# Latent chunks ahead of context chunks in one input norm, one-pass factors for the mixer's two norms, and column sums kept in one bank

## What is computed

```python
def rms_norm(x, g):
    y = xf * lax.rsqrt(jnp.mean(xf * xf, axis=-1, keepdims=True) + EPS)
    return (y * g).astype(x.dtype)
# second layer
h_lat = modulate(rms_norm(lat, norm1_g[1]), sh1, sc1)
h_ctx = modulate(rms_norm(cx, norm1_g[1]), csh1, csc1)
z_lat = h_lat @ w_in                       # queries need latents only
kv_ctx = h_ctx @ w_in[:, C_Q_LORA:]        # keys and values need both
...
return rms_norm(lat, final_g)              # end of the first block ("final1")
...
h = rmsnorm(x, norm_mix_g[0])              # start of the second ("mix"), x being that result
proj = h @ w_in[0]
```

## Time and profile before

| | us |
|---|---|
| median of 3 runs | 1631.31 (1631.01 to 1636.09) |
| the profiled execution | 1633.56 |
| its span, first to last instruction | 1631.7 |
| PE busy in it | 1535.8 (94%) |
| DVE busy | 1126.5 (69%) |
| ACT busy | 797.4 (49%) |
| mean granted TensorE clock | 0.973 |

### The profile page before, as it was taken

How to read it: one execution, slowest core, us unless ns; L and a number is a source line. 1 busy time by engine, 2 the same in 40 slices (tenths; PEclk the granted TensorE clock), 3 DMA queues, 4 the chain that set the end, 5 groups by cost and what they waited for, 6 DMA issues and landing times.

```text
span 1631.7 us, 31148 instructions
## 1 busy us (share of the span) xinstructions
PE 1535.8 (94%) x11566; PEld 1355.6 (83%) x11566; DVE 1126.5 (69%) x1853; ACT 797.4 (49%) x1437; POOL 122.9 (8%) x139
## 2 busy tenths in 40 slices
PE   5899988899899999999899999999999889999998
PEld 3688878787688888878786799999898669999997
DVE  5986866544798888887735478875666755577653
ACT  2545554243544545322445567765445455666542
POOL 2000052512000000010000010001000001000000
PEclk8999999899899999999899999999899999999999
DMA  9354520002244445566431045556454214255552
GB/s 368 108 180 164 186 66 2 3 2 78 94 177 170 165 166 179 174 213 217 173 110 52 5 151 190 183 197 214 144 168 143 84 59 143 92 191 182 186 188 90
DMA packets 62957, 230.80 MB, mean 141 GB/s; under 512 B 6800, under 2 KB 8080, under 8 KB 62352
## 3 DMA queue, kind: packets, MB, share of 16 engines
q1 hardware_dynamic: 61408, 223.37, 39.5%
q0 software_dynamic: 1168, 5.80, 1.0%
q10 hardware_dynamic: 288, 0.33, 0.1%
HBM read 228.43 MB, written 1.05 MB: 141 GB/s over the span
## 4 chain that ended last, share of the span: by engine, by line
PE 85%; DVE 8%; ACT 4%; issue 2%; DMA 1%; POOL 1%; DVEq 0%; ACTq 0%; POOLq 0%
PE proj L662 23%; PE proj L663 23%; PE proj L664 23%; PE bank L714 1%; PE bank L925 1%; DVE w_low L2165 1%; ACT w_high L1647 1%; PE proj L1145 1%; DMA ident_sb<-ident 1%; PE bank L942 1%; PE bank L972 1%; POOL tmp L1516 1%; PE proj L1147 1%; PE proj L1146 1%; PE bank L1160 1%
## 5 line engine op out<-in xcount | busy, mean ns | idle before, releaser
L662 PE MATMUL proj<-h_high,w_high 128*128 128x256 f32 (+1 forms) x1776 | 583.0, 328 | 19.9 <-DVE h_low L2198 13.5
L663 PE MATMUL proj<-h_low,w_high 128*128 128x256 f32 (+1 forms) x1776 | 572.0, 322 | 0.0
L664 PE MATMUL proj<-h_high,w_low 128*128 128x256 f32 (+1 forms) x1776 | 570.6, 321 | 0.0
L2165 DVE TENSOR_TENSOR w_low<-w_raw,w_high 128x1024 fp32r<-128x1024 f32 x322 | 393.3, 1224 | 152.9 <-ACT w_high L1647 151.5
L1647 ACT ACTIVATE w_high<-w_raw 128x1024 fp32r<-128x1024 f32 x322 | 337.9, 1054 | 232.0 <-PE proj L664 228.0
L662 PEld LDWEIGHTS proj<-h_high,w_high 128*128 128x128 f32 x1776 | 337.2, 190 | 56.5 <-issue 18.4
L664 PEld LDWEIGHTS proj<-h_high,w_low 128*128 128x128 f32 x1776 | 337.8, 190 | 27.2
L663 PEld LDWEIGHTS proj<-h_low,w_high 128*128 128x128 f32 x1776 | 337.5, 190 | 24.4
L662 PE MATMUL proj<-act_high,w_high 128*128 128x256 f32 (+1 forms) x608 | 190.6, 313 | 0.1
L663 PE MATMUL proj<-act_low,w_high 128*128 128x256 f32 (+1 forms) x608 | 189.7, 312 | 0.0
L664 PE MATMUL proj<-act_high,w_low 128*128 128x256 f32 (+1 forms) x608 | 189.3, 311 | 0.0
(11 more groups left out here) (413 smaller groups left out, 1911.2 us busy)
## 6 DMA issues: line engine op xcount, KB each, us to landing
w_raw<-w_stream SPq DMA_DIRECT2D x322, 512.0 KB, 3.3
a_ring<-a_stream SPq DMA_DIRECT2D x80, 512.0 KB, 4.1
a_first<-a_head SPq DMA_DIRECT2D x4, 1024.0 KB, 18.0
a_first<-a_stream SPq DMA_DIRECT2D x4, 1024.0 KB, 18.6
x<-x_in SPq DMA_DIRECT2D x1, 2048.0 KB, 10.3
late_tab<-late_tables POOLq DMA_DIRECT2D x1, 1408.0 KB, 6.6
cond_rows<-cond_rows SPq DMA_DIRECT2D x1, 1024.0 KB, 5.6
cond_rows<-cond_rows POOLq DMA_DIRECT2D x1, 1024.0 KB, 5.1
```

Of the source, the lines that this page charges most:

```text
L662: mm(out_, wh, xh, start=first, stop=False)
L663: mm(out_, wh, xl, start=False, stop=False)
L664: return mm(out_, wl, xh, start=False, stop=last)
L2165: v.tensor_tensor(wl(n), RAW[:, n % 4, :], wh(n), ALU.subtract).then_inc(w_low, 1)
```

## The change

**n1_1 by stream.** `norm_parts` lists 16 parts for the names in `BY_STREAM` (only n1_1): eight latent chunks, then eight context chunks, each of 256 columns, with a count of their own. Tiles 0 to 2 wait for the latents only, tile 3 waits for each context chunk. On ACT block in1+2 is split ahead of the root, and tile copies and splits stand between the context chunks. On DVE the `w_low` of in1+2 follows context chunk 0 and that of in1+3 follows context chunk 4 (`beside`). POOL's load of `mem_in` waits for all 16.

**One bank of sums.** `norm_sum` puts the columns of all token groups side by side in one bank, only the very first matmul opening the accumulation, and `norm_root` takes one square root over the 2 or 4 columns, for every norm.

**The mixer's factor.** With s the mean of x squared, the two factors together are 1/sqrt(mean(x²·(g²+eps)) + eps²), g being `final1`'s weight. So ACT squares x scaled by sqrt(g²+eps), held in eight new columns of `small` that two linked ACT instructions make at the start of dn1, and both factors become a root and a reciprocal each, without the other. PE sums chunk by chunk for both names (`mix` in bank 0, `final1` in bank 2) and spreads them apart, `mix` into bank 0 and `final1` into bank 1, with a signal each. The first index logits of in2_v, which use bank 1, wait until `X` is scaled. Column `eps_squared` fills the padding of `cols_sb`; `small` grows from 72 to 88 columns, so every buffer behind it lies 64 bytes higher.

```diff
-            for t in range(width // P):
-                last = f(STD[:, t:t + 1], SUMS[t][:, 0:1], ACT.Sqrt, scale=1.0 / features, bias=col("eps"))
-            last.then_inc(n_root, 1)
+            nt = width // P
+            f(STD[:, 0:nt], BK[0][:, 0:nt], ACT.Sqrt, scale=1.0 / features, bias=col("eps")).then_inc(n_root, 1)
...
+        def norm_parts(name):
+            nch = NORMS[NORM_I[name]][1]
+            if name in BY_STREAM:
+                return [(k, [part]) for part in ((LAT, 1), (CTX, 0)) for k in range(nch)]
+            return [(k, streams(name)) for k in range(nch)]
...
             norm_start("mix" if then == "final1" else then)
+            if then == "final1":
+                link(f(SM[:, 72:80], C[:, COL_AT["final1"]:COL_AT["final1"] + KC], ACT.Square))
+                link(f(SM[:, 72:80], SM[:, 72:80], ACT.Sqrt, bias=col("eps")))
...
-            if then != "final1" and then not in UNSCALED:
+            if then in BY_STREAM:
+                split(B0["in1"] + 2)
+                norm_root(then)
+                norm_high(then, range(KC))
+            elif then != "final1" and then not in UNSCALED:
                 norm_end(then)
...
-        split(B0["in1"] + 2)
+        norm_high("n1_1", range(KC, KC + 3))
         for m, o in enumerate([CQ[:, 0, :], CQ[:, 1, :], CQ[:, 2, :], CKV[:, 0, :], CKV[:, 1, :], KR[:]]):
             split(B0["in1"] + m + lead("in1"))
+            if m == 2:
+                norm_high("n1_1", range(KC + 4, 2 * KC))
             done(T0["in1"] + m)
             f(o, PL[(T0["in1"] + m) % 2][:, 0:o.shape[1]], ACT.Copy).then_inc(tile_out, 1)
+            if m == 0:
+                norm_high("n1_1", range(KC + 3, KC + 4))
...
-            norm("n1_1")
-            low(B0["in1"] + 2)
-            rest("in1", 0, 4)
+            norm("n1_1", lambda j: low(B0["in1"] + 2 + (j > KC)) if j in (KC, KC + 4) else None)
+            rest("in1", 1, 4)
...
-            norm_sum("mix", 1, 0)
-            norm_sum("final1", 0, 2)
-            pe.wait_ge(n_std, NORM_I["mix"] + 2)
+            norm_sum("mix", "final1")
+            for c, name in enumerate(("mix", "final1")):
+                pe.wait_ge(n_std, NORM_I[name] + 1)
...
+                    if c == 0:
+                        pe.wait_ge(n_xn, NORM_X0["final1"] + KC)
...
-            for t in range(2):
-                last = v.scalar_tensor_tensor(STD[:, 16 + t:17 + t], SUMS[t][:, 1:2], STD[:, 8 + t:9 + t], STD[:, 8 + t:9 + t], ALU.mult, ALU.mult)
```

More of the change, by code:

```diff
@@ L42 @@
         ("a_ln_g", 4), ("a_ln_b", 4), ("b_norm", 1), ("mla_q", 3), ("mla_kv", 2), ("fconv", 2 * 2 * FC * 3),
-        ("final1", 8), ("mix", 8), ("kv2", 1), ("cross", 8), ("mem", 8), ("mlp", 8), ("final2", 8), ("eps", 1), ("one", 1)]
+        ("final1", 8), ("mix", 8), ("kv2", 1), ("cross", 8), ("mem", 8), ("mlp", 8), ("final2", 8), ("eps", 1), ("one", 1), ("eps_squared", 1)]
 COL_AT = {}
@@ L88 @@
 UNSCALED = ("cross", "mlp")
+BY_STREAM = ("n1_1",)
 NORM_X0 = {}
 NORM_C0, NORM_S0 = {}, {}
-_c = _s = 0
+_c = _s = _x = 0
 for _name, _nc, _ in NORMS:
-    NORM_C0[_name], NORM_S0[_name] = _c, _s
-    NORM_X0[_name] = _c - sum(n for m, n, _ in NORMS[:NORM_I[_name]] if m in UNSCALED)
+    NORM_C0[_name], NORM_S0[_name], NORM_X0[_name] = _c, _s, _x
+    _parts = 2 * _nc if _name in BY_STREAM else _nc
     _c += _nc
-    _s += _nc if _name in SPLIT else 0
+    _x += 0 if _name in UNSCALED else _parts
+    _s += _parts if _name in SPLIT else 0
 A_FIRST = 16
@@ L672, in free_bank, with tile @@
                 pe.wait_ge(tile_out, t + 1 + off)
-            def tile(n, t, x, width, off=0):
+            def tile(n, t, x, width, off=0, ready=None):
                 weights(n, off)
@@ L700, in h_ready, with norm_sum @@
                 return lambda k: (n_lo, NORM_S0[name] + k + 1)
-            def norm_sum(name, c=0, count=1):
-                _, nch, width = NORMS[NORM_I[name]]
-                chunks = [0, *range(EARLY, nch)] if name in SUMMED else range(nch)
+            def norm_sum(*names):
+                _, nch, width = NORMS[NORM_I[names[0]]]
+                early = names[0] in SUMMED
+                chunks = [0, *range(EARLY, nch)] if early else range(nch)
                 for k in chunks:
-                    if name in SUMMED and k == 0:
-                        pe.wait_ge(n_early, (EARLY - 1) * (SUMMED.index("final1" if name == "mix" else name) + 1))
-                    else:
-                        pe.wait_ge(n_sq, sq_count(name, k))
-                    for t in range(width // P):
-                        last = mm(SUMS[t][:, c:c + 1], squares(name, k)[:, t * P:(t + 1) * P], ONES[:, 0:1], start=(k == 0), stop=(k == nch - 1))
-                if count:
-                    last.then_inc(n_ss, count)
+                    for c, name in enumerate(names):
+                        if early and k == 0:
+                            pe.wait_ge(n_early, (EARLY - 1) * (SUMMED.index(names[-1]) + 1))
+                        else:
+                            pe.wait_ge(n_sq, sq_count(name, k))
+                        for t in range(width // P):
+                            o = BK[2 * c][:, t:t + 1]
+                            last = mm(o, squares(name, k)[:, t * P:(t + 1) * P], ONES[:, 0:1], start=(k == 0 and t == 0), stop=(k == nch - 1 and t == width // P - 1))
+                        if k == nch - 1:
+                            last.then_inc(n_ss, 1)
             def norm_spread(name):
@@ L1103, in _ @@
                 x = LAT if m < 3 else slice(0, T2)
-                tile(B0["in1"] + m, T0["in1"] + m, x, SEQ if m < 3 else T2)
+                ready = (lambda k: (n_lo, NORM_S0["n1_1"] + KC + k + 1)) if m == 3 else None
+                tile(B0["in1"] + m, T0["in1"] + m, x, SEQ if m < 3 else T2, ready=ready)
                 if m == 3:
@@ L2202, in low_part @@
                     last.then_inc(n_lo, 1)
-                for k in range(nch):
+                for j, (k, own) in enumerate(parts):
                     src = norm_src(name, k)
```

78 lines of the change are left out of this document (39 added, 39 removed).

## The result

The changed kernel takes 1636.84 us (1635.69 to 1638.18, 8 runs) against 1631.16 (1627.79 to 1636.09, 8 runs) for the kernel before: ratio 1.0032, 95% interval 1.0019 to 1.0044. That is 5.7 us slower, where 8.9 us faster was forecast. The profiled execution took 1635.69 us; its span is 1633.9.

The account below looks back on a forecast made before the run. TensorE, 85% of the chain, was taken as the bound, other engines counting only where it waits. Terms -0.42 - 0.42 - 4.1 - 0.22 + 0.45 - 4.2 = -8.9 us gave 1622.4 us on the median, range 1619 to 1628.5.

Parts of the forecast that it names:

- n1_1: Second layer's input norm: order by stream starts projections and third tile earlier; 4.1 us gain, root's 0.42 included, bounds 1.5 to 4.9.
- One bank of sums: All norms: column sums put into neighbouring columns of one bank cost nothing, bound 0.02 us a pass either way.
- The mixer: Mixer's norms: sums, root and spread finish sooner, so scaling starts earlier; 4.2 us gain, bounds 2.5 to 5.3.
- the address shift: Rival, all projections: activations 64 bytes higher might slow matmuls; at 1% 6.5 us slower than before, 1637.8; chance 0.08.
- One root: Norms: one root for four or two saves 0.42 us at n1_0, n2_0, n1_1 each, 0.11 at n2_1, final2 each.
- The queue of ScalarE: At n1_1: copy behind rounding and split starts third tile at 805.2; rival: handovers delay it near 808, chance 0.12.
- The rival with the halved clock: At n1_1's third tile: clock halves in the pause, so n1_1 gains only 2.0 us, total 1624.5; chance 0.20.
- Start of dn1: Two added small ScalarE instructions, covered by nothing, delay TensorE by 0.45 us, bounds 0.2 to 0.7.
- The new wait in in2_v: First index logits wait until `X` is scaled; VectorE's work covers it by 2.1 us, so it costs nothing.

Follow-up runs that it names:

- two distances: Unshifted changed kernel with ScalarE's tile 0 copy earlier, `w_high` at distance 0 ahead of in1 and 192 from in1 on; 1614.65 us, ratio 0.9899 to before.

## Why the prediction was wrong, step by step

**The step that failed** is the one that left the address shift out of the sum. It stood among the rivals, with the right quantity in it (slower from 0.6% per matmul on), and got 0.08 because no row showed a price and the alignment stayed legal. "No row shows it" was true of the trace of before, but bounds were due on either side: the range, 1619 to 1628.5, was added up from the bounds of the other terms, and no slower case lies in it. The page of the changed kernel shows how much hangs on the operands' place, and that of before had the same counts (one of three such groups for each operand; x the number of matmuls, then busy us and mean ns of one):

```profile
L663 PE MATMUL proj<-h_high,w_high 128*128 128x256 f32 (+1 forms) x1776 | 587.6, 331 | 17.5 <-DVE h_low L2223 11.0
...
L663 PE MATMUL proj<-act_high,w_high 128*128 128x256 f32 (+1 forms) x608 | 192.8, 317 | 0.8 <-DVE w_low L2188 0.8
```

That is three times 2384, so 7152 of 11566 matmuls; at 1% a matmul no other term of the sum is as large. Measured, it is 1.5% at 512 columns and 1.0% at 256, and 12.5 to 14.7 us. The rival's own figure, 1637.8, is 1 us off, in part by luck: it took 1% on all of TensorE's busy time.

**The size of the rest was right, partly by luck.** Unshifted, the change takes 1622.12 us; the forecast was 1622.4. But the aligned starts of that kernel give only 0.4 us at n2_0 (0.4 to 0.5 in every changed kernel, nothing in the copies of before), 1.8 in n1_1, 3.6 at the mixer and 0.1 at n2_1, and lose 0.6 at dn1: about 5.3. The root's 0.45 at n1_0 shows in three other traces and can't be read in this one; the 0.2 at final2 is no more than what copies of before show there. So the traces bear out 5 to 6 us of the 8.9, and what is left of the 9.6 lies where executions differ anyway. A second kernel with the same order, higher by 256, is at 1624.91, 7.7 us under before.

**One root.** Right in size. The changed kernel, ACT, answering to the earlier trace rows:

```profile
795.58 0.26 ACT L1685 ACTIVATE std<-bank,cols_sb 128x4 f32<-128x4 f32 x1 [0.20 <-PE bank L720]
```

It takes 0.26 against 0.72 for four, and 0.26 again for two columns at the mixer. From the root's start to the spread's the time is 0.60 us (795.58 to 796.18) against 1.05 (792.25 to 793.30): 0.45, forecast 0.42. The Trainium skill ("ScalarE: Activation LUTs", Rules for kernel authors) budgets about 0.3 us for one; the trace agrees for a lone one. As a price for each of four it does not hold here: three fewer would have given 0.9 us.

**n1_1: -2.9 where -4.1 was said,** and -1.8 in the unshifted kernel. PE of the changed kernel from the sums to the end of the fourth tile, answering to the earlier trace rows:

```profile
792.60 2.94 PE L720 MATMUL bank<-ones,squares_n 128*128 128x1 f32 x24
796.18 2.07 PE L728 MATMUL bank<-ident_sb,std 128*128 128x128 f32 x8 [0.64 <-DVE std L2207]
...
799.98 0.55 PE L663 MATMUL proj<-h_high,w_high 128*128 128x256 f32 x1 [1.73 <-DVE h_low L2223]
...
809.57 0.36 PE L663 MATMUL proj<-h_high,w_high 128*128 128x256 f32 x1 [0.98 <-ACT cq L1992]
...
818.06 1.40 PE L720 MATMUL bank<-ones,tmp 128*128 128x1 f32 x12
```

Its first scaling on DVE, answering to the first of the earlier trace rows:

```profile
798.29 0.87 DVE L2234 SCALAR_TENSOR_TENSOR tmp<-x,gains,bank 128x256 f32<-128x256 f32 x2 [2.17 <-PE bank L728]
```

Before, PE's sums and spread were:

```profile
789.27 2.94 PE L714 MATMUL bank<-ones,squares_n 128*128 128x1 f32 x24
793.30 1.16 PE L722 MATMUL bank<-ident_sb,std 128*128 128x128 f32 x8 [1.09 <-DVE std L2184]
```

From the first scaling to the first projection: 1.69 us, forecast 1.69. To the third tile: 11.28, forecast 11.13 (805.2 - 794.07), before 14.82. The queue of ScalarE was followed rightly through eleven parts, a split and a copy, and the pause ahead of the third tile is there, ended by the copy as said (0.98 us, where 1.3 to 2.7 was said). The term that was missed is ahead of all that: the eight matmuls that spread the factors take 2.07 us and not 1.16, so the first scaling comes 5.69 after the first sum and not 5.22 - 0.42. They are the same matmuls; the clock differs. Stretch of the spread in the changed kernel (PE, PEld, DVE, ACT, POOL, PEclk, DMA), the granted clock being the lower level, 1.2 GHz:

```profile
796.00:798.20 2.20, 2.02 (x8) 1.78 (x8) 0.12 (x1) 0.00 (x0) 0.00 (x0) 0.50 0.90 369
```

The prediction looked at the clock over the 4 us from the spread's start on (0.66 on the earlier trace rows) and took the spread itself at before's speed. Nor is that the root's fault: the kernel before, run again, shows the slow spread in its own order:

```profile
792.23 2.02 PE L722 MATMUL bank<-ident_sb,std 128*128 128x128 f32 x8 [1.09 <-DVE std L2184]
```

So the profiled execution of before had happened to run it fast, and 0.9 us of the forecast gain was a property of one execution. The kernel without the order by stream had it at 1.16, the unshifted one at 1.79.

The rival with the halved clock did occur, in other executions. PE of the unshifted changed kernel at its third tile, then the stretches behind it:

```profile
799.17 0.36 PE L663 MATMUL proj<-h_high,w_high 128*128 128x256 f32 x1 [1.93 <-ACT cq L1992]
```

```profile
799.17:801.17 2.00, 2.00 (x13) 2.00 (x14) 1.72 (x3) 2.00 (x4) 0.00 (x0) 0.72 0.00 0
801.17:803.60 2.43, 2.43 (x14) 2.43 (x13) 1.88 (x6) 1.72 (x4) 0.00 (x0) 0.53 0.55 182
```

The kernel higher by 256 shows the same pause and the same fall. The pause is 1.93 us in both and 0.98 in the changed kernel, whose third tile stays at the upper level:

```profile
809.57:812.40 2.83, 2.83 (x24) 2.83 (x25) 2.01 (x3) 2.83 (x6) 0.00 (x0) 1.00 0.00 0
```

The third tile takes 4.43 us in the one (799.17 to 803.60) and 2.8 in the other. In the changed kernel the first tiles had run longer at the lower level (24 matmuls, to 805.5), while the copy came at the same time after the first scaling, so less pause was left; the kernel higher by 192 paused 1.45 us and stayed at the upper level too. Whether the addresses have a part in that is not shown. With the copy ahead of two rounding steps and the split, the third tile starts 9.7 us behind the first scaling (24 matmuls counted back from its end at 806.95; the first scaling is at 794.41) with no pause. ScalarE's copy of tile 0, then PE's fourth tile, in that kernel:

```profile
803.26 0.38 ACT L1993 ACTIVATE cq<-proj 128x256 f32<-128x256 f32 x1 [1.65 <-PE proj L665]
```

```profile
807.49 0.51 PE L663 MATMUL proj<-h_high,w_high 128*128 128x512 f32 x1 [0.38 <-DVE w_low L2191]
```

The next wait is the `w_low` of in1+3, 0.38 us.

**Start of dn1: right.** ACT in the changed kernel, answering to the earlier trace rows:

```profile
1092.00 0.20 ACT L1669 ACTIVATE small<-cols_sb 128x1 f32<-128x1 f32 x1
1092.11 0.19 ACT L1725 ACTIVATE small<-cols_sb 128x8 f32<-128x8 f32 x1
1092.34 0.30 ACT L1726 ACTIVATE small<-small,cols_sb 128x8 f32<-128x8 f32 x1
1092.67 2.95 ACT L1661 ACTIVATE w_high<-w_raw 128x1024 fp32r<-128x1024 f32 x3
```

From the first small instruction to the splits it takes 0.67 us, before 0.11; TensorE lost 0.54 (0.45 forecast), and 0.58 in the unshifted kernels.

**The mixer: -3.4 to -3.6 where -4.2 was said.** The second and the last row of before to compare are the spread at 1152.67 and the first projection at 1156.32. PE of the changed kernel, then, from the timeline of DVE, the first scaling:

```profile
1150.10 2.73 PE L720 MATMUL bank<-ones,tmp 128*128 128x1 f32 x24
1153.00 1.37 PE L1262 MATMUL bank<-ident_sb,std 128*128 128x128 f32 x8 [0.17 <-DVE std L2252]
1155.29 0.55 PE L663 MATMUL proj<-h_high,w_high 128*128 128x256 f32 x1 [0.91 <-DVE h_low L2259]
```

```profile
1153.75 0.87 DVE L2256 SCALAR_TENSOR_TENSOR tmp<-x,small,bank 128x256 f32<-128x256 f32 x2 [0.43 <-PE bank L1262]
```

The spread starts 2.90 us behind the first sum, forecast 2.8 (1149.7 - 1146.92), before 5.75. Scaling follows 0.75 behind it at a mean granted share of 0.70, 4.2 us earlier behind the first sum than before, and that is the forecast to the tenth; the first projection follows 1.54 behind it. What failed is what comes next. The clock now stays at the lower level until well into the projections (stretches of the changed kernel):

```profile
1153.00:1155.00 2.00, 1.37 (x8) 1.07 (x8) 1.32 (x4) 0.86 (x3) 0.30 (x1) 0.70 0.89 318
...
1157.30:1159.30 2.00, 2.00 (x11) 2.00 (x11) 2.00 (x7) 1.07 (x4) 0.00 (x0) 0.50 0.04 8
1159.30:1161.30 2.00, 2.00 (x14) 2.00 (x13) 1.33 (x3) 1.27 (x2) 0.00 (x0) 0.67 0.00 0
```

It rises between 1159.3 and 1161.3, 4 to 6 us behind the first projection (1155.29); before it was up from about 1159.7 on, 3.4 us behind it; 0.8 us of the 4.2 went there by the aligned starts. In the unshifted kernel the clock rises earlier, but the spread itself ran at the lower level (2.08 us for eight matmuls), and the scaling came 0.5 later. The prediction had both as bounds (up to 1.7 for a late rise) and took neither.

**The new wait in in2_v: right.** DVE ends scaling `X` at 1228.89, and PE comes to the first index logits 2.1 us later, without idle time, as in the earlier trace rows:

```profile
1227.24 1.65 DVE L2722 SCALAR_TENSOR_TENSOR x<-x,cols_sb,bank 128x256 f32<-128x256 f32 x4
```

```profile
1231.01 0.49 PE L1287 MATMUL bank<-proj 64*128 64x128 f32 x4
```

**One bank of sums: right.** 24 passes of n1_1 take 2.94 us in both.

## To carry to other kernels

Before a buffer is made longer, look at what lies behind it: an edit that moves the operands of the busiest engine is an edit of every instruction that reads them, and it is tested alone, by padding the kernel before, ahead of anything else. Compare the number of matmuls that fit a saturated stretch before and after: it tells a slower matmul from a longer wait. And where a term of a sum rests on the time of a few matmuls next to a pause, take it at both clock levels, since one profiled execution shows only one of them.

## What the runs showed of the hardware

The speed of these fp32 matmuls depends on where the moving rows lie against the stationary weights, modulo 256 bytes. By the distance of rows minus `w_high`, averages over a stretch:

| distance | 512 columns, us each | 256 columns, us each | shown by |
|---|---|---|---|
| 64 | 0.2289 | 0.1178 | before; before all moved; changed, unshifted and higher by 256 |
| 128 | 0.2324 to 0.2333 | 0.1190 | changed; before shifted by 64; before, all behind `tmp` higher |
| 192 | 0.2333 | 0.1156; 0.1139 with `w_low2` too | before shifted by 128; two distances (256 columns only) |
| 0 | 0.2267 | 0.1194 | changed, higher by 192; before, weights higher by 64 |

The ends are 3% apart at 512 columns and 5% at 256, and no single distance is best for both. The Trainium skill ("SBUF — State Buffer", A bandwidth-pool intuition that's wrong) gives TensorE a port for the moving operand and a second, independent one for the weight load; from that alone a reader would not expect the one's address to matter against the other's. The runs here say that it does, by 12.5 us in 1631.

What stays open: why. The distance is not all of it. The changed kernel and before shifted by 64 have every buffer at the same place, and from 450 to 590 us the one has a matmul every 0.2324 us and the other every 0.2333. The spacing isn't even within a stage either. In before shifted by 64 the four blocks of up1 have a matmul every 0.1188, 0.1188, 0.1185 and 0.1200 us, and the last two read the same pair of buffers, at the same distances, from its two slots; in before all four are at 0.1178. Distances that are no multiple of 64 were tried on `w_low2` alone: at 224 and at 32, with the other weights at 64, its blocks stay at 0.1175 to 0.1178, at 96 they lose what distance 192 gives the others. Whether the two reads meet in the memory, or something else does, was not taken apart.
